# Flip before the scores, low parts before the maximum, three value passes in the forgetting attention

## The chip, the cores and the metric

The kernel runs on one core of a Trainium2 chip. The metric is the device time of one execution in microseconds; the time quoted is the median of the runs. All arithmetic is float32: TensorE (PE in the profile) reads float32 operands that are split by the program into a high part rounded to fp32r and a low part, the rest, and adds the products of the parts.

## The reference

One layer of a streaming encoder: half a SwiGLU block, a token mix with two groups of eight attention heads, and half a second SwiGLU block, with RMS norms around each. It runs on 1024 prompt rows and on 128 sample rows (8 streams of 16 with caches of 512). The change touches the two attentions of the prompt:

```python
s = einsum('bqhd,bkhd->bhqk', q, k) * scale        # scores of one head
if decay: s = s + (lq[t] - lk[s])                  # group B: forgetting attention (FoX)
s = where(mask, s, -inf)                           # block-causal (MLA) or per frame (FoX)
p = softmax(s, axis=-1)
out = einsum('bhqk,bkhd->bqhd', p, v)              # v has 64 columns per head
```

## The kernel before

The stages follow one another with a barrier between: feed-forward 1 with the input projection, latents, `mla_prompt`, `sample_setup`, `sample_attention`, `fox_prompt`, output projection, feed-forward 2. Each stage is five instruction lists written out by hand (PE; ACT, the scalar engine; DVE, the vector engine; POOL, GpSimd; SP, the sync engine for DMAs). Each engine works through its list in order, and semaphores tie the lists together.

`mla_prompt` (L1459) and `fox_prompt` (L1774) have the same skeleton. A head has PT = 8 row tiles of 128 queries. Row g = 8·n + t is tile t of head n; being causal, it has t + 1 key tiles. The parts of a row are:

- `score(g)` on PE writes the scores into one of two PSUM buffers; it waits for the exponentials of row g - 2, which read the same buffer.
- `maximum(g)` on DVE takes the row maximum, `exponent(g)` on ACT the exponentials into `p` (the one ACTIVATE of L1635 and L1955, with its sum read out after it).
- `flip_row(g)` on PE transposes `p` tile by tile into the two PSUM buffers of `flip`, in groups of at most four tiles (tiles 4 to 7 of a head have two groups); group x waits for `pt_lo` of group x - 2, its buffer's last reader.
- `weights_high(g)` on ACT copies a group out of PSUM as the high part, and `weights_low(g)` on DVE subtracts it from PSUM to give the low part.
- `prep`, `high`, `low` turn and split the queries and keys of head n + 1, one piece at each of t = 1, 2, 3, 4 (`PREP_STEP`). In `fox_prompt` POOL copies each high part a second time (`double`).
- `values(n, h, ...)` on PE multiplies the transposed weights of half h by V: half 0 of head n at t = 6, 7, half 1 at t = 0 to 3 of the next head. The stationary operand `vv` holds V's high and low parts side by side (128 columns), so two passes (weights high, weights low) give both in one PSUM bank: high·V in partitions 0 to 63, low·V in 64 to 127. ACT copies the upper half out (`take_low`), DVE adds it to the lower (`copy_out`), at t = 0 and t = 4.

The order around the change, in the loop over g (L1603, L1635 on; L1928 on in `fox_prompt`), LEAD = 2:

```
PE :  score(g+2)    flip_row(g)      prep, values
DVE:  maximum(g+2)  weights_low(g)   low, copy_out, invert
ACT:  weights_high(g)  exponent(g+2) high, v_high, take_low
```

In the last head of `fox_prompt`, at t = 0, ACT also issues the eight DMAs of `load_w_out`.

Of the kernel before, what the change touches and what calls it, by code (L numbers as in the profile page):

```python
# [8 lines left out]
P = 128  # L9
# [45 lines left out]
def plain(ap):  # L55

    return ap.bitcast(F32)
# [176 lines left out]
H = 8  # L234
# [1224 lines left out]
def mla_prompt(nc, ident, ident_bf, mask_bf, q_rows, kv_rows, krope, acc, early_hi, early_lo, inverse_out, load_next, limit):  # L1459
# [8 lines left out]
    with Tools(nc, "mla") as k:  # L1468
# [43 lines left out]
        with k.block() as block:  # L1512
# [17 lines left out]
            def _(pe):  # L1530
# [72 lines left out]
                keys(1)  # L1603
                for g in range(-LEAD, ROWS):
                    n, t = divmod(g, PT)
                    if g + LEAD < ROWS:
                        score(g + LEAD)
                    if g >= 0:
                        flip_row(g)
                        if n + 1 < H and t in PREP_STEP:  # L1610
                            prep(n + 1, PREP_STEP[t])
                        if n and t in PV_LATE:
                            values(n - 1, 1, PV_LATE[t])
                        if t in PV_EARLY:
                            values(n, 0, PV_EARLY[t])
# [65 lines left out]
            @block.vector  # L1681
            def _(dve):
                def low(n, r):
                    src, hi, lo, factor = part(n, r)
                    dve.wait_ge(hi_ok, PREP * n + r + 1)
                    dve.scalar_tensor_tensor(lo, src, factor, plain(hi), ALU.mult, ALU.subtract).then_inc(lo_ok, 1)

                def key_low(hf):
                    cols = slice(hf * HALF, hf * HALF + HALF)
                    dve.wait_ge(key_hi, hf + 1)  # L1690
                    dve.tensor_tensor(kT_lo[0][NOPE:QW, cols], key_bank(hf), plain(kT_hi[0][NOPE:QW, cols]), ALU.subtract).then_inc(key_lo, 1)

                def maximum(g):
                    n, t = divmod(g, PT)
                    dve.wait_ge(scored, g + 1)
                    dve.tensor_reduce(nmax[:, g:g + 1], scores[:, g % 2, 0:(t + 1) * P], axis=AX.X, op=ALU.max, negate=True).then_inc(maxed, 1)

                def weights_low(g):
                    hi, lo, cols = weights(g)
                    for x, k0, k1 in groups_of(g):  # L1700
                        dve.wait_ge(pt_hi, x + 1)
                        dve.tensor_tensor(lo[:, k0:k1, cols], flip[:, x % 2, 0:(k1 - k0) * P].rearrange("p (k n) -> p k n", n=P), plain(hi[:, k0:k1, cols]), ALU.subtract).then_inc(pt_lo, 1)

                def invert(n):
# [12 lines left out]
                low(0, 1)  # L1717
                key_low(0)
                low(0, 2)
                low(0, 3)  # L1720
                key_low(1)
                for g in range(-LEAD, ROWS):
                    n, t = divmod(g, PT)
                    if g + LEAD < ROWS:
                        maximum(g + LEAD)
                    if g >= 0:
                        weights_low(g)
                        if n + 1 < H and t in PREP_STEP:
# [45 lines left out]
def fox_prompt(nc, ident, ident_bf, mask_bf, decay, rows, loaded, acc, v_parts, decayT, inverse_out, load_next):  # L1774
# [11 lines left out]
    with Tools(nc, "fox") as k:  # L1786
# [1 line left out]
        p = k.sb("p", [P, NP_ROWS, SEQ])  # L1788
        early_hi, early_lo = [k.sb(f"early_{n}", [P, HT, HALF], F32R) for n in ("hi", "lo")]
        late_hi, late_lo = [k.sb(f"late_{n}", [P, PT, HALF], F32R) for n in ("hi", "lo")]  # L1790
        vv, low_rows, o_raw, scale_rows = v_parts
        nmax, total = [k.sb(n, [P, ROWS]) for n in ("nmax", "total")]
        inverse = k.sb("inverse", [P, 2, PT])
        scores = k.ps("scores", [P, 2, SEQ])
# [1 line left out]
        turn = k.ps("turn", [P, HALF])  # L1796
        out = k.ps("out", [P, HALF])
        pT_hi, pT_lo = (early_hi[:, :, :], late_hi[:, :, :]), (early_lo[:, :, :], late_lo[:, :, :])
        out_of = (turn, out)
        turned, hi_ok, lo_ok, doubled = k.sem("turned"), k.sem("hi_ok"), k.sem("lo_ok"), k.sem("doubled")  # L1800
        ones_ok, decay_turned, decay_taken = k.sem("ones_ok"), k.sem("decay_turned"), k.sem("decay_taken")
        decay_in = [k.sem(f"decay_in{b}") for b in range(2)]
        scored, maxed, exped, inverted = k.sem("scored"), k.sem("maxed"), k.sem("exped"), k.sem("inverted")
        inverse_at, scale_in, o_copied = k.sem("inverse_at"), k.sem("scale_in"), k.sem("o_copied")
        flipped, pt_hi, pt_lo = k.sem("flipped"), k.sem("pt_hi"), k.sem("pt_lo")
        v_hi_ok, v_lo_ok, pv_ok, low_out, o_taken = k.sem("v_hi_ok"), k.sem("v_lo_ok"), k.sem("pv_ok"), k.sem("low_out"), k.sem("o_taken")

        def turn_bank(n, r):

# [20 lines left out]
        with k.block() as block:  # L1830
# [29 lines left out]
            def _(pe):  # L1860
# [43 lines left out]
                def values(n, h, pieces):  # L1904
                    b = n % 2
                    for c in pieces:
# [8 lines left out]
                        c0 = max(0, c - HT * h) * P  # L1915
                        dst = out_of[h][:, c0:HALF]
                        high, low = pT_hi[h][:, c, c0:HALF], pT_lo[h][:, c, c0:HALF]
                        pe.matmul(dst, vv[b][:, c, :], high, start=(c == 0), stop=False)
                        last = pe.matmul(dst, vv[b][:, c, :], low, start=False, stop=(c == HT * (h + 1) - 1))
                        if c == HT * (h + 1) - 1:  # L1920
                            last.then_inc(pv_ok, 1)

# [4 lines left out]
                    prep(0, r)  # L1927
                for g in range(-LEAD, ROWS):  # L1928
                    n, t = divmod(g, PT)
                    if g + LEAD < ROWS:  # L1930
                        score(g + LEAD)
                    if g >= 0:
                        flip_row(g)
                        if n + 1 < H and t in PREP_STEP:
                            prep(n + 1, PREP_STEP[t])
                        if n and t in PV_LATE:
# [6 lines left out]
            def _(act):  # L1943
# [19 lines left out]
                        act.wait_ge(flipped, x + 1)  # L1963
                        act.activation(hi[:, k0:k1, cols], flip[:, x % 2, 0:(k1 - k0) * P].rearrange("p (k n) -> p k n", n=P), ACT.Copy).then_inc(pt_hi, 1)

                def take_low(n, h):
                    act.wait_ge(pv_ok, 2 * n + h + 1)
                    if n or h:
                        act.wait_ge(o_copied, 2 * n + h)
                    act.activation(low_rows, out_of[h][VD:P, :], ACT.Copy).then_inc(low_out, 1)  # L1970

                def v_high(n):
                    if n >= 2:
                        act.wait_ge(pv_ok, 2 * (n - 1))
                    if n == 0:
                        act.wait_ge(loaded[1], 16)
                    act.activation(vv[n % 2][:, :, 0:VD], v_rows(n), ACT.Copy).then_inc(v_hi_ok, 1)

                for hf in range(HALVES):
                    act.wait_ge(decay_turned, hf + 1)  # L1980
# [3 lines left out]
                for g in range(-LEAD, ROWS):  # L1984
# [5 lines left out]
                    if g >= 0:  # L1990
                        if n + 1 < H and t in PREP_STEP:
                            high(n + 1, PREP_STEP[t])
                        if t == V_STEP:
                            v_high(n)
                        if n and t == EARLY_OUT_STEP:
                            take_low(n - 1, 0)
                        if n and t == LATE_OUT_STEP:
                            take_low(n - 1, 1)
                        if n == H - 1 and t == 0:
                            act.wait_ge(turned, PREP * H)  # L2000
                            load_next(act)
                for h in range(HALVES):
                    take_low(H - 1, h)

            @block.vector
            def _(dve):
# [20 lines left out]
                    dve.reciprocal(inverse[:, n % 2, :], total[:, PT * n:PT * n + PT]).then_inc(inverted, 1)  # L2027

                def copy_out(n, h):
                    dve.wait_ge(low_out, 2 * n + h + 1)  # L2030
                    if n:
                        dve.wait_ge(o_taken, 2 * n + h - 1)
                    dve.tensor_tensor(o_raw[:, h, :], out_of[h][0:VD, :], low_rows, ALU.add).then_inc(o_copied, 1)

                for b in range(2):
                    dve.memset(plain(q_tail[b][64:TAIL, :]), 1.0).then_inc(ones_ok, 1)
# [2 lines left out]
                    low(0, r)  # L2039
                for g in range(-LEAD, ROWS):  # L2040
                    n, t = divmod(g, PT)
                    if g + LEAD < ROWS:
                        maximum(g + LEAD)
                    if g >= 0:
                        weights_low(g)
                        if n + 1 < H and t in PREP_STEP:
                            low(n + 1, PREP_STEP[t])
                        if n and t == EARLY_OUT_STEP:
# [9 lines left out]
            def _(pool):  # L2058
# [12 lines left out]

                def v_low(n):
                    pool.wait_ge(v_hi_ok, n + 1)
                    pool.tensor_tensor(vv[n % 2][:, :, VD:2 * VD], v_rows(n), plain(vv[n % 2][:, :, 0:VD]), ALU.subtract).then_inc(v_lo_ok, 1)

                for r in range(PREP):
                    double(0, r)
# [668 lines left out]
def layer(nc, x_prompt, x_sample, cache_ckv, cache_krope, cache_fk, cache_fv, cache_logf, g1_pre, g1_post, w1_gu, w1_down,  # L2746
# [14 lines left out]
    with Tools(nc, "all") as k:  # L2761
# [55 lines left out]
        with Tools(nc, "mix") as m:  # L2817
# [46 lines left out]
            with Tools(nc, "dec_all") as d:  # L2864
# [5 lines left out]
                fox_prompt_rows = [fox_q.take("rows0", [P, PT, FW])] + [fox_kv.take(f"rows{n}", [P, PT, FW]) for n in (1, 2)]  # L2870
                sample_setup(nc, ident, q_rows[:, PT, :], select, setup_in, load_first_keys, own)
                sample_attention(nc, ident, ident_bf, mask_bf[:, 2 * P:2 * P + NEW], pair_pick[:, :], own, cache_ckv, cache_krope, cache_fk, cache_fv, fox_rows, ckv_out, acc, fox_prompt_rows, fox_loaded, keys_in, tri[:, :], ones[:, :], logf, decay)
                fox_v = Region(nc, "fox_v", xT_at + 2 * PT * FW * 4, 4 * PT * VD * 4 + HALF * 4)
                fox_o = Region(nc, "fox_o", xT_at + 63488, 2 * SEQ * 4)
                v_parts = [[fox_v.take(f"vv{b}", [P, PT, 2 * VD], F32R) for b in range(2)], fox_v.take("low_rows", [VD, HALF])[:, :], fox_o.take("raw", [VD, HALVES, HALF]), fox_o.take("scale_rows", [VD, SEQ])]
                decayT = nc.alloc_sbuf_tensor_at("decayT", [4 * H, SEQ], F32R, offset=places_end + PT * FW * 4)
                fox_prompt(nc, ident, ident_bf, mask_bf[:, P:2 * P], decay, fox_prompt_rows, fox_loaded, acc, v_parts, decayT,
                           inverse_rows[1], lambda eng: [load_w_out(eng, w_out, w_out_raw, c, w_out_at) for c in range(KD)])
# [53 lines left out]
```

## Time and profile before

| | us |
|---|---|
| median of 3 runs | 2577.03 (2576.94 to 2579.33) |
| the profiled execution's own time | 2577.59 |
| its span in the trace | 2575.8 |
| `mla_prompt`, first to last exponential | 1112.7 to 1285.1 |
| `fox_prompt`, first to last exponential | 1456.4 to 1635.5 |

| engine | busy us | share |
|---|---|---|
| PE (matmul) | 2349.7 | 91% |
| DVE | 1547.3 | 60% |
| ACT | 997.5 | 39% |
| POOL | 820.9 | 32% |

Busy shares are means over all the stages. The two feed-forward blocks are most of the span; the change lies in two stages of some 190 us each, whose own rows stand below.

### The profile page before, as it was taken

The page shows a single profiled execution, that of the slowest core. Times are in us where ns is not written, and L with a number is a line of the kernel's source. Part 1 is how long each engine was busy: PE and PEld are TensorE (multiplying, and loading weights), DVE is VectorE, ACT ScalarE, POOL GpSimd, SP SyncE. Part 2 cuts the span into 40 slices and gives each one's busy share as a digit, 9 for nine tenths or more (in the row PEclk, how much of TensorE's full clock was granted, in tenths as well). Part 3 has the DMA queues.
Part 4 walks back from the last instruction along what each step waited for, and adds up shares of the span by engine and source line. Part 5 has one row for each costly group of instructions (what it writes and reads, how often), then busy time and mean ns, then how long its engine had stood idle before and what let it go on. Part 6 is the DMA issues. An engine that isn't in the chain of part 4 may idle for free. (4 is left out here: it accounts for less than half of the span.)

```text
span 2575.8 us, 41219 instructions
## 1 busy us (share of the span) xinstructions
PE 2349.7 (91%) x14523; PEld 2108.0 (82%) x14523; DVE 1547.3 (60%) x2502; ACT 997.5 (39%) x2013; POOL 820.9 (32%) x647
## 2 busy tenths in 40 slices
PE   5999999999989999878889878796999999999985
PEld 4999999998867789767766666685999999998864
DVE  7766666655587223366643566666766666655565
ACT  6222222233454112466633366534322222233443
POOL 1544444434461000012221032223444444434452
PEclk8999999999999999899989888897999999999998
DMA  4444444367564221010054200223344444456663
GB/s 151 126 151 131 150 141 158 125 202 239 185 220 165 104 72 39 24 38 9 13 214 160 84 10 14 107 98 98 101 158 141 141 145 135 144 190 211 199 208 134
DMA packets 247809, 330.90 MB, mean 128 GB/s; under 512 B 34416, under 2 KB 141040, under 8 KB 245648
## 3 DMA queue, kind: packets, MB, share of 16 engines
q1 hardware_dynamic: 246544, 325.26, 38.4%
q10 hardware_dynamic: 1152, 4.19, 0.4%
q8 instruction: 63, 1.03, 0.2%
q14 instruction: 50, 0.41, 0.0%
HBM read 234.51 MB, written 94.75 MB: 128 GB/s over the span
## 5 line engine op out<-in xcount | busy, mean ns | idle before, releaser
L62 PE MATMUL ffn_bank<-x_hi,ffn_w_w_hi 128*128 128x256 f32 (+1 forms) x2464 | 736.0, 299 | 24.4 <-DVE x_lo L969 23.8
L63 PE MATMUL ffn_bank<-x_lo,ffn_w_w_hi 128*128 128x256 f32 (+1 forms) x2464 | 734.1, 298 | 0.0
L64 PE MATMUL ffn_bank<-x_hi,ffn_w_w_lo 128*128 128x256 f32 (+1 forms) x2464 | 734.0, 298 | 0.0
L62 PEld LDWEIGHTS ffn_bank<-x_hi,ffn_w_w_hi 128*128 128x128 f32 x2464 | 472.4, 192 | 27.0 <-DVE x_lo L969 26.2
L63 PEld LDWEIGHTS ffn_bank<-x_lo,ffn_w_w_hi 128*128 128x128 f32 x2464 | 472.7, 192 | 0.0
L64 PEld LDWEIGHTS ffn_bank<-x_hi,ffn_w_w_lo 128*128 128x128 f32 x2464 | 472.3, 192 | 0.0
L738 POOL TENSOR_TENSOR ffn_split_dn_lo<-ffn_in_dn_raw,ffn_split_dn_hi 128x512 fp32r<-128x512 f32 x176 | 250.7, 1429 | 289.1 <-ACT ffn_split_dn_hi L805 283.5
L724 POOL TENSOR_TENSOR ffn_w_w_lo<-gu_raw,ffn_w_w_hi 128x512 fp32r<-128x512 f32 x176 | 239.6, 1362 | 300.3 <-ACT ffn_w_w_hi L755 300.1
L1001 DVE TENSOR_TENSOR ffn_split_a_lo<-ffn_in_a_raw,ffn_split_a_hi 128x512 fp32r<-128x512 f32 (+2 forms) x176 | 218.5, 1257 | 176.2 <-ACT ffn_split_a_hi L807 176.1
L62 PE MATMUL ffn_bank<-ffn_split_dn_hi,ffn_split_a_hi 128*128 128x512 f32 x704 | 278.7, 396 | 22.8 <-DVE ffn_split_a_lo L1001 18.7
L724 POOL TENSOR_TENSOR ffn_w_w_lo<-ffn_w_s,ffn_w_w_hi 128x512 fp32r<-128x512 f32 x132 | 192.8, 1462 | 299.6 <-ACT ffn_w_w_hi L755 299.6
L63 PE MATMUL ffn_bank<-ffn_split_dn_lo,ffn_split_a_hi 128*128 128x512 f32 x704 | 276.5, 393 | 0.0
L64 PE MATMUL ffn_bank<-ffn_split_dn_hi,ffn_split_a_lo 128*128 128x512 f32 x704 | 276.3, 392 | 0.0
L755 ACT ACTIVATE ffn_w_w_hi<-ffn_w_s 128x512 fp32r<-128x512 f32 x132 | 83.4, 632 | 377.6 <-DVE ffn_w_s L915 298.4
L805 ACT ACTIVATE ffn_split_dn_hi<-ffn_in_dn_raw 128x512 fp32r<-128x512 f32 x176 | 110.9, 630 | 275.5 <-PE ffn_bank L64 223.5
L755 ACT ACTIVATE ffn_w_w_hi<-gu_raw 128x512 fp32r<-128x512 f32 x176 | 110.1, 627 | 276.2 <-PE ffn_bank L64 273.8
L62 PEld LDWEIGHTS ffn_bank<-ffn_split_dn_hi,ffn_split_a_hi 128*128 128x128 f32 x704 | 133.5, 190 | 58.8 <-POOL ffn_split_dn_lo L738 23.4
L960 DVE TENSOR_TENSOR ffn_w_a_st<-ffn_w_u,ffn_w_gate 128x320 f32<-128x320 f32 (+1 forms) x176 | 167.6, 991 | 0.1
L64 PEld LDWEIGHTS ffn_bank<-ffn_split_dn_hi,ffn_split_a_lo 128*128 128x128 f32 x704 | 133.7, 190 | 27.9
L63 PEld LDWEIGHTS ffn_bank<-ffn_split_dn_lo,ffn_split_a_hi 128*128 128x128 f32 x704 | 133.6, 190 | 27.1
L62 PE MATMUL ffn_bank<-in_hi,all_xT_hi 128*128 128x512 f32 (+2 forms) x360 | 131.3, 365 | 6.6 <-DVE all_xT_lo L181 6.6
L63 PE MATMUL ffn_bank<-in_lo,all_xT_hi 128*128 128x512 f32 (+2 forms) x360 | 130.7, 363 | 0.0
(420 smaller groups left out, 4031.0 us busy)
## 6 DMA issues: line engine op xcount, KB each, us to landing
gu_raw<-in_w_ffn_gu SPq DMA_DIRECT2D x88, 512.0 KB, 5.2
ffn_w_w_raw<-in_w_ffn_down SPq DMA_DIRECT2D x22, 1024.0 KB, 4.9
a_rows<-ffn_w_a_st SPq DMA_DIRECT2D x44, 512.0 KB, 2.8
t_rows<-ffn_w_w_raw SPq DMA_DIRECT2D x88, 256.0 KB, 2.3
s_rows<-ffn_w_a_st SPq DMA_DIRECT2D x88, 256.0 KB, 2.4
ffn_in_dn_raw<-in_w_ffn_down SPq DMA_DIRECT2D x88, 256.0 KB, 3.5
ffn_in_dn_raw<-t_rows SPq DMA_DIRECT2D x88, 256.0 KB, 2.8
ffn_in_a_raw<-s_rows SPq DMA_DIRECT2D x88, 256.0 KB, 3.0
```

The source lines that it names most:

```text
L62: pe.matmul(out, w_hi, x_hi, start=first, stop=False)
L63: pe.matmul(out, w_hi, x_lo, start=False, stop=False)
L64: return pe.matmul(out, w_lo, x_hi, start=False, stop=last)
L724: pool.tensor_tensor(w_lo[n][:, :, :], raw, plain(w_hi[n][:, :, :]), ALU.subtract).then_inc(w_lo_ok, 1)
L738: pool.tensor_tensor(dn_lo[e][:, :], dn_raw[r][:, :], plain(dn_hi[e][:, :]), ALU.subtract).then_inc(dn_lo_ok, 1)
L755: act.activation(w_hi[n][:, :, :], raw, ACT.Copy).then_inc(w_hi_ok, 1)
L805: act.activation(dn_hi[e][:, :], dn_raw[r][:, :], ACT.Copy).then_inc(dn_hi_ok, 1)
L960: dve.tensor_tensor(a_st[at.b][:, col:col + CW[c]], up[c][:, :], gate[c][:, :], ALU.mult).then_inc(prod_ok, 1)
L1001: dve.tensor_tensor(a_lo[e][:, c0:c1], a_raw[r][:, c0:c1], plain(a_hi[e][:, c0:c1]), ALU.subtract).then_inc(a_lo_ok, 1)
```

## The change

In both stages PE flips row g before it computes the scores of row g + 2, and DVE subtracts the low parts of row g before it takes the maximum of row g + 2. ACT's list keeps its order. In `fox_prompt` alone V's high and low parts get tensors of their own with 64 columns each; the value products are three passes (V high by weights high, V high by weights low, V low by weights high) into 64 partitions, `take_low` is gone, and `copy_out` copies from PSUM when the products are done. The small product low by low is no longer formed there.

```diff
@@ mla_prompt and fox_prompt, PE
                     n, t = divmod(g, PT)
+                    if g >= 0:
+                        flip_row(g)
                     if g + LEAD < ROWS:
                         score(g + LEAD)
                     if g >= 0:
-                        flip_row(g)
                         if n + 1 < H and t in PREP_STEP:
@@ mla_prompt and fox_prompt, DVE
+                    if g >= 0:
+                        weights_low(g)
                     if g + LEAD < ROWS:
                         maximum(g + LEAD)
                     if g >= 0:
-                        weights_low(g)
@@ fox_prompt, values
-                        pe.matmul(dst, vv[b][:, c, :], high, start=(c == 0), stop=False)
-                        last = pe.matmul(dst, vv[b][:, c, :], low, start=False, stop=(c == HT * (h + 1) - 1))
+                        pe.matmul(dst, v_hi[b][:, c, :], high, start=(c == 0), stop=False)
+                        pe.matmul(dst, v_hi[b][:, c, :], low, start=False, stop=False)
+                        last = pe.matmul(dst, v_lo[b][:, c, :], high, start=False, stop=(c == HT * (h + 1) - 1))
@@ fox_prompt, ACT: take_low and its four calls
-                def take_low(n, h):
-                    act.wait_ge(pv_ok, 2 * n + h + 1)
-                    if n or h:
-                        act.wait_ge(o_copied, 2 * n + h)
-                    act.activation(low_rows, out_of[h][VD:P, :], ACT.Copy).then_inc(low_out, 1)
@@ fox_prompt, DVE: copy_out
-                    dve.wait_ge(low_out, 2 * n + h + 1)
+                    dve.wait_ge(pv_ok, 2 * n + h + 1)
...
-                    dve.tensor_tensor(o_raw[:, h, :], out_of[h][0:VD, :], low_rows, ALU.add).then_inc(o_copied, 1)
+                    dve.tensor_copy(o_raw[:, h, :], out_of[h]).then_inc(o_copied, 1)
```

The rest of the diff names the two new tensors in `v_high`, `v_low` and `layer`.

## Rows read from the trace of the kernel before

**Rows 1.** Busy time by window: window, length, each engine's busy us (count), PEclk, DMA.
```profile
1110.00:1286.00 176.00, 146.71 (x907) 122.47 (x908) 120.61 (x209) 121.17 (x272) 34.23 (x24) 0.95 0.06 19
1456.00:1636.00 180.00, 141.13 (x807) 115.70 (x806) 118.49 (x205) 118.08 (x269) 48.51 (x50) 0.87 0.10 35
1591.50:1593.00 1.50, 1.50 (x8) 1.50 (x9) 0.29 (x2) 0.87 (x3) 1.42 (x2) 0.50 0.00 0
```
**Rows 2.** Waits from 1456 to 1636: who waited for whom, us, times, longest.
```profile
ACT fox_p L1955 <- DVE fox_nmax L2015: 27.8, 43, 2.2
PE fox_flip L1901 <- DVE fox_late_lo L2021: 22.3, 16, 3.0
```
**Rows 3.** Timeline, ACT, one head of fox_prompt: start, us, line, operation [idle before].
```profile
1569.62 0.36 ACT L1955 ACTIVATE fox_p<-fox_scores,fox_nmax 128x128 f32<-128x128 f32 x1
...
1573.46 0.47 ACT L1955 ACTIVATE fox_p<-fox_scores,fox_nmax 128x256 f32<-128x256 f32 x1
...
1574.79 0.58 ACT L1955 ACTIVATE fox_p<-fox_scores,fox_nmax 128x384 f32<-128x384 f32 x1 [0.48 <-DVE fox_nmax L2015]
...
1577.43 0.69 ACT L1955 ACTIVATE fox_p<-fox_scores,fox_nmax 128x512 f32<-128x512 f32 x1 [0.69 <-DVE fox_nmax L2015]
...
1580.30 0.80 ACT L1955 ACTIVATE fox_p<-fox_scores,fox_nmax 128x640 f32<-128x640 f32 x1 [0.24 <-DVE fox_nmax L2015]
...
1583.28 0.90 ACT L1955 ACTIVATE fox_p<-fox_scores,fox_nmax 128x768 f32<-128x768 f32 x1 [0.51 <-DVE fox_nmax L2015]
...
1584.17 0.58 ACT L1947 ACTIVATE fox_q_both<-fox_turn 64x512 fp32r<-64x512 f32 x1
1584.65 0.62 ACT L1977 ACTIVATE fox_v_vv<-fox_x_rows 128x512 fp32r<-128x512 f32 x1
...
1586.62 1.01 ACT L1955 ACTIVATE fox_p<-fox_scores,fox_nmax 128x896 f32<-128x896 f32 x1 [0.71 <-DVE fox_nmax L2015]
...
1590.70 1.11 ACT L1955 ACTIVATE fox_p<-fox_scores,fox_nmax 128x1024 f32<-128x1024 f32 x1 [0.98 <-DVE fox_nmax L2015]
...
1593.56 0.36 ACT L1955 ACTIVATE fox_p<-fox_scores,fox_nmax 128x128 f32<-128x128 f32 x1
```
**Rows 4.** Timeline of the same head, DVE and PE.
```profile
1577.85 0.40 PE L1918 MATMUL fox_out<-fox_late_hi,fox_v_vv 128*128 128x512 f32 x1
1578.09 0.40 PE L1919 MATMUL fox_out<-fox_late_lo,fox_v_vv 128*128 128x512 f32 x1
...
1584.78 0.68 DVE L2010 SCALAR_TENSOR_TENSOR fox_q_both<-fox_turn,fox_q_both 64x512 fp32r<-64x512 f32 x1 [0.94 <-ACT fox_q_both L1947]
...
1585.49 1.09 DVE L2015 TENSOR_REDUCE fox_nmax<-fox_scores 128x1 f32<-128x896 f32 x1
...
1591.41 1.73 PE L1901 MATMUL fox_flip<-all_ident,fox_p 128*128 128x128 f32 x7 [2.99 <-DVE fox_late_lo L2021]
```
**Rows 5.** Groups by form from 1456 to 1636: busy us, mean ns, idle before.
```profile
L2021 DVE TENSOR_TENSOR fox_late_lo<-fox_flip,fox_late_hi 128x512 fp32r<-128x512 f32 x37 | 25.3, 685 | 17.0 <-ACT fox_late_hi L1964 16.5
L1964 ACT ACTIVATE fox_late_hi<-fox_flip 128x512 fp32r<-128x512 f32 x37 | 21.9, 594 | 19.1 <-PE fox_flip L1901 18.9
...
L2021 DVE TENSOR_TENSOR fox_early_lo<-fox_flip,fox_early_hi 128x128 fp32r<-128x128 f32 x8 | 2.3, 282 | 0.0
...
L2015 DVE TENSOR_REDUCE fox_nmax<-fox_scores 128x1 f32<-128x128 f32 x8 | 2.2, 276 | 0.7 <-PE fox_scores L1893 0.7
```
**Rows 6.** Timeline, ACT, mla_prompt: row 7 of head 2, then rows 0, 1.
```profile
1174.61 1.11 ACT L1635 ACTIVATE mla_p<-mla_scores,mla_nmax 128x1024 f32<-128x1024 f32 x1 [0.99 <-DVE mla_nmax L1696]
...
1176.85 0.37 ACT L1635 ACTIVATE mla_p<-mla_scores,mla_nmax 128x128 f32<-128x128 f32 x1
...
1179.09 0.48 ACT L1635 ACTIVATE mla_p<-mla_scores,mla_nmax 128x256 f32<-128x256 f32 x1
```
**Rows 7.** Timeline, ACT, mla_prompt: row 7 of head 6, four heads later.
```profile
1266.12 1.11 ACT L1635 ACTIVATE mla_p<-mla_scores,mla_nmax 128x1024 f32<-128x1024 f32 x1 [0.99 <-DVE mla_nmax L1696]
```
**Rows 8.** Timeline, ACT's DMA issues in the last head of fox_prompt.
```profile
1623.60 3.00 ACTq L2626 DMA_DIRECT2D w_out_raw<-in_w_out  x6
```

More of the change, by code:

```diff
@@ L1790, in fox_prompt @@
         late_hi, late_lo = [k.sb(f"late_{n}", [P, PT, HALF], F32R) for n in ("hi", "lo")]
-        vv, low_rows, o_raw, scale_rows = v_parts
+        v_hi, v_lo, o_raw, scale_rows = v_parts
         nmax, total = [k.sb(n, [P, ROWS]) for n in ("nmax", "total")]
@@ L1798, in fox_prompt @@
         pT_hi, pT_lo = (early_hi[:, :, :], late_hi[:, :, :]), (early_lo[:, :, :], late_lo[:, :, :])
-        out_of = (turn, out)
+        out_of = (turn[0:VD, :], out[0:VD, :])
         turned, hi_ok, lo_ok, doubled = k.sem("turned"), k.sem("hi_ok"), k.sem("lo_ok"), k.sem("doubled")
@@ L1805, in fox_prompt @@
         flipped, pt_hi, pt_lo = k.sem("flipped"), k.sem("pt_hi"), k.sem("pt_lo")
-        v_hi_ok, v_lo_ok, pv_ok, low_out, o_taken = k.sem("v_hi_ok"), k.sem("v_lo_ok"), k.sem("pv_ok"), k.sem("low_out"), k.sem("o_taken")
+        v_hi_ok, v_lo_ok, pv_ok, o_taken = k.sem("v_hi_ok"), k.sem("v_lo_ok"), k.sem("pv_ok"), k.sem("o_taken")
         def turn_bank(n, r):
@@ L1929, in _ @@
                     n, t = divmod(g, PT)
+                    if g >= 0:
+                        flip_row(g)
                     if g + LEAD < ROWS:
@@ L1932, in _ @@
                     if g >= 0:
-                        flip_row(g)
                         if n + 1 < H and t in PREP_STEP:
@@ L1976, in v_high @@
                         act.wait_ge(loaded[1], 16)
-                    act.activation(vv[n % 2][:, :, 0:VD], v_rows(n), ACT.Copy).then_inc(v_hi_ok, 1)
+                    act.activation(v_hi[n % 2][:, :, :], v_rows(n), ACT.Copy).then_inc(v_hi_ok, 1)
                 for hf in range(HALVES):
@@ L1994, in _ @@
                             v_high(n)
[L1995 to L1998, printed above, removed]
                         if n == H - 1 and t == 0:
@@ L2001, in _ @@
                             load_next(act)
-                for h in range(HALVES):
-                    take_low(H - 1, h)
             @block.vector
@@ L2041, in _ @@
                     n, t = divmod(g, PT)
+                    if g >= 0:
+                        weights_low(g)
                     if g + LEAD < ROWS:
@@ L2073, in v_low @@
                     pool.wait_ge(v_hi_ok, n + 1)
-                    pool.tensor_tensor(vv[n % 2][:, :, VD:2 * VD], v_rows(n), plain(vv[n % 2][:, :, 0:VD]), ALU.subtract).then_inc(v_lo_ok, 1)
+                    pool.tensor_tensor(v_lo[n % 2][:, :, :], v_rows(n), plain(v_hi[n % 2][:, :, :]), ALU.subtract).then_inc(v_lo_ok, 1)
                 for r in range(PREP):
@@ L2872, in layer @@
                 sample_attention(nc, ident, ident_bf, mask_bf[:, 2 * P:2 * P + NEW], pair_pick[:, :], own, cache_ckv, cache_krope, cache_fk, cache_fv, fox_rows, ckv_out, acc, fox_prompt_rows, fox_loaded, keys_in, tri[:, :], ones[:, :], logf, decay)
-                fox_v = Region(nc, "fox_v", xT_at + 2 * PT * FW * 4, 4 * PT * VD * 4 + HALF * 4)
+                fox_v = Region(nc, "fox_v", xT_at + 2 * PT * FW * 4, 4 * PT * VD * 4)
                 fox_o = Region(nc, "fox_o", xT_at + 63488, 2 * SEQ * 4)
-                v_parts = [[fox_v.take(f"vv{b}", [P, PT, 2 * VD], F32R) for b in range(2)], fox_v.take("low_rows", [VD, HALF])[:, :], fox_o.take("raw", [VD, HALVES, HALF]), fox_o.take("scale_rows", [VD, SEQ])]
+                v_parts = [[fox_v.take(f"{n}{b}", [P, PT, VD], F32R) for b in range(2)] for n in ("hi", "lo")] + [fox_o.take("raw", [VD, HALVES, HALF]), fox_o.take("scale_rows", [VD, SEQ])]
                 decayT = nc.alloc_sbuf_tensor_at("decayT", [4 * H, SEQ], F32R, offset=places_end + PT * FW * 4)
```

1 line of the change is left out of this document (removed).

## The prediction

> **What bounds the kernel now.** I read the busy times by window first. Both attention stages keep PE at about 80% of the time, DVE and ACT at 65 to 70% each [rows 1]: no engine is full, so a chain through several engines sets the pace. Nothing beside these stages can take up a change: each ends in a barrier, and what they gain or lose is lost or gained in the total, one for one.
>
> The waits say which chain. ACT waits 27.8 us for the maximum in 43 places, and PE waits 22.3 us for low parts, up to 3.0 us at a time [rows 2]. The timeline of one head then gives the eight steps, each from the start of one exponential to that of the next: row 0 to 1 3.84, 1 to 2 1.33, 2 to 3 2.64, 3 to 4 2.87, 4 to 5 2.98, 5 to 6 3.34, 6 to 7 4.08, 7 to the next 0 2.86; sum 23.94 us [rows 3]. In the exponentials of rows 2 to 7 ACT waits for the maximum. The chain of step 5 to 6 can be read off: exponential at 1583.28, ACT's high part of the next head's queries at 1584.17, DVE's low part of it at 1584.78, the maximum at 1585.49, then the exponential at 1586.62 [rows 3, 4]. The flipped weights are not in it: ACT copies the high part of row g and goes on to `exponent(g+2)`, while DVE subtracts row g's low part beside that exponential. That is the overlap which the present order buys.
>
> Two steps are of another kind. Before row 6 is flipped PE stands still for 2.99 us, waiting for row 5's low parts, which are queued behind the 1.21 us maximum of row 7. Seven transposes then take 1.73 us and the granted clock is 0.50, the 1.2 GHz level [rows 1, 4]. The steps 7 to 0 and 0 to 1 run in that state: 2.86 + 3.84 = 6.70 us. The same steps in the multi-head latent stage at a head where the clock did not stay low are 2.24 + 2.24 = 4.48 us [rows 6]. So the low clock costs the forgetting stage 2.2 us a head. The latent stage has 22.88 us a head, from four heads between rows 7 of head 2 and head 6 [rows 6, 7].
>
> **The change, part by part.** *The order on PE.* Flipping row g ahead of the scores of row g + 2 lets ACT take the high part earlier, by the scores' 0.3 to 1.2 us (up to four matmuls of 0.24 from start to start [rows 4]; an estimate for the smaller ones). The scores come later by the transposes, 0.11 each at the full clock, an estimate from half of 1.73/7. Neither is on the new chain below except through it.
>
> *The order on DVE.* This is the costly edit. ACT's list still says high(g), exponent(g+2). DVE's now says low(g), maximum(g+2). So maximum(g+2) cannot start before ACT has copied high(g) and DVE has subtracted it, and exponent(g+2), which stands right behind high(g), waits for both. What ran side by side becomes one file: exponential, (next head's piece on ACT and DVE), high, low, maximum, exponential. Behind the waiting exponential ACT holds the next head's high piece and high(g+1), and for these wait DVE and, through its buffers, PE.
>
> I write this file out for a head. Instructions on ACT start 0.10 before the one in front ends (0.58 to 0.48 in the pair at 1584.17), on DVE 0.08 before; a hop between the two costs 0.03. An exponential with its read-out holds ACT for its own length. High parts: 0.28, 0.38, 0.49, 0.60 for 128 to 512 columns; low parts 0.28, 0.41, 0.55, 0.69, the inner ones on the straight line between the rows; the maximum 0.28 plus 0.134 for each further tile [rows 3, 4, 5].
>
> - 7 to 0: 1.11 + high 0.60 + hop 0.03 + low 0.61 + 0.47 + maximum 0.28 + 0.03 = 3.13
> - 0 to 1: 0.36 + 0.60 + 0.03 + 0.61 + 0.61 + 0.41 + 0.03 = 2.65
> - 1 to 2: 0.47 + 0.28 + 0.03 + 0.20 + 0.54 + 0.03 = 1.55
> - 2 to 3: 0.58 + 0.38 + 0.03 + 0.33 + 0.68 + 0.03 = 2.03
> - 3 to 4: 0.69 + piece high 0.58 + 0.03 + piece low 0.61 + low 0.47 + 0.81 + 0.03 = 3.22 (high runs beside the piece's low)
> - 4 to 5: 0.80 + 0.58 + 0.03 + 0.61 + 0.61 + 0.94 + 0.03 = 3.60
> - 5 to 6: 0.90 + piece 0.48 + V high 0.52 + high 0.60 + 0.03 + low 0.61 + 0.20 + 1.08 + 0.03 = 4.45
> - 6 to 7: 1.01 + 0.58 + 0.03 + 0.61 + copy_out 0.61 + low 0.61 + 0.33 + 1.21 + 0.03 = 5.02
>
> The sum is 25.65 us, against 23.94: 1.7 more in the forgetting stage, although it has no slow PE in it yet. Steps 3 to 7 lose 3.0 (16.29 for 13.27), steps 7 to 1 win 0.9 and steps 1 to 3 0.4.
>
> *What stays of the low clock.* PE's stop ahead of row 6 does not go. Row 6 waits for low(5), which now stands before the maximum but behind exponential 6 on ACT, the piece, both high parts and copy_out: PE has nothing left after the scores of row 0, about 3 us again. So I expect the half clock after it, as now. But PE has slack there: row 6's transposes end about 1 us before ACT is free for their high part. Of the 2.2 us I keep 1.0 in the forgetting stage (bounds: 0 if the slack takes all, 2.2 if none). A head is 26.6, or 2.7 more than before.
>
> *The latent stage* has the same file, and keeps `take_low`. At step 2 to 3 that puts ACT's 0.6 and DVE's copy_out behind each other, 0.8 more: 26.45, against 22.88: 3.6 more a head. Bounds on the clock there: 0 and again 2.2, if the stop, 2.7 now, gets longer and the clock stays down as long as in the other stage; I take 0 because the slack covers the short form of it.
>
> *Three value passes.* A head has 4608 columns of weights in each pass (1280 for half 0, 3328 for half 1). At 0.24 for 512 the third costs PE 2.1 us a head, 17 in all [rows 4]. The cover is PE's own idle time: 141 us busy in 180 [rows 1] is 18.8 in a head of 23.94, so 21 in one of 26.6. I count 0 inside and 1 at the end of the stage, where the last half runs alone; without the cover it would be 17. Taking `take_low` out relieves ACT of 16 copies of 0.6 (9.5 us). At t = 4 it is worth nothing, for DVE's piece and copy_out stand in the file anyway; at t = 0 it is the 0.8 that the latent stage has and this one has not, which the sum holds already. The new copy I cost as the addition that it replaces; bounds 0.3 to 0.7 for each of 16, of which 8 are in the file: 0 to -3.
>
> *The ends.* The last head has no pieces, but its low parts go into the file: 0.2 + 0.33 + 0.47 + 0.61 + 0.81 + 0.94 for t = 0 to 5, 3.4 us, of which I take 3. In the forgetting stage ACT issues the eight loads there, six of them in 3.00 us [rows 8]; before, the stall of ACT had DVE's maximum done beside it, now high, low and maximum follow it: 1.5 more.
>
> *Sum.* Forgetting stage: 7 heads by 2.7 = 19, the last head 3 + 1.5, the value tail 1: 24. Latent stage: 7 by 3.6 = 25, the last head 3: 28. Together 52. On the profiled execution's own 2577.6 (span 2575.8) that is 2629.6; the median of the runs lies 0.6 lower, so 2629.
>
> **The rivals.**
> *PE spends more of each head at the low level.* For it: in the forgetting stage the mean clock is 0.87 already [rows 1], and in the new order PE is idle for a larger part, 21 of 26.6 us busy (0.79) there and about 19.5 of 26.45 (0.74, now 0.83) in the latent stage. Against: stops of under 1 us, of which both kernels have several a head, leave the clock alone at present. At the half rate PE's matmuls of a step go above the file's length; if the low stretch doubles, each head pays the whole 2.2 again in both stages: 15 by 2.2 = 33 above my sum, 2662. The Trainium skill, TensorE: Matmul & The Clock Gate, Part 1, says that the throttled state is the default and that activity releases it; by that rule an emptier PE speaks for this rival. Here the rows agree with it as far as one stop of 2.99 us and the 0.50 behind it go, and show nothing of a PE that is merely less busy.
>
> *The order is neutral and the third pass is bare.* If DVE's two jobs only change places in a cycle that PE bounds, then the reordering costs nothing, and the 17 us of matmuls come on top: 2577 + 17 = 2594. Against it stand the waits of ACT for the maximum; PE is never what they end on.
>
> *The other side: faster.* One mechanism: the stop before row 6. In the new order low(5) no longer waits for the 1.21 us maximum of row 7. If the stop shrinks from 2.99 to under 2 us, and with it the low clock goes, steps 7 to 1 fall to 4.5 us: 2.2 by 7 = 15 in this stage, and 1 by 7 in the latent one (an estimate: its mean clock of 0.95 lies less than half as far below full as the other's 0.87 [rows 1]), 2577 - 22 = 2555. It decides only if low(g) ahead of the maximum costs ACT nothing, that is if high(g) were early enough to have low(g) done before the scores of g + 2. At t = 5 high(5) stands on ACT behind exponential 6 and a piece, so the low parts cannot be early; I give it little.
>
> **How the numbers follow.** The file as forecast: 0.80. More low clock: 0.10. Neutral order with a bare pass: 0.05. Faster: 0.03. No change, the edits evening out: 0.02. A measurement of this kernel tells 0.2%, 5 us, from no change. Faster 0.03, same 0.02, slower 0.95. Range: the lower bounds (no clock cost in the forgetting stage, 7 less; the cheaper copy, 3; half a microsecond a head of work that hides after all, 8) give 2611; the upper ones (2.2 for 1.0 there, 8; 2.2 in half of the latent heads, 8; the rival's further part) reach 2658. I set 2609 to 2660.
>
> **What would show it.** Right: in a head the steps 3 to 7 are longer by 0.3 to 1.1 each and the low part stands directly before the maximum on DVE; the wait of ACT for the maximum about doubles in both stages; steps 5 to 6 and 6 to 7 near 4.4 and 5.0; PE's stop ahead of row 6 is still there. Wrong: exponentials that start without waiting for the maximum, PE at over 90% in these stages (the neutral rival), a granted clock of 1.0 throughout a head (the faster one), or below 0.8 as a mean of the stage (the first one).

## The result and the profile after

The changed kernel takes 2629.4 us (2626.7 to 2631.3), the one before 2577.0: a ratio of 1.0205, 95% interval 1.0182 to 1.0228. The forecast was 2629.

The busy time by window, in the columns of [rows 1]: the latent stage, the forgetting stage, and 1.5 us behind the stop ahead of row 6 of a forgetting head.

```profile
1110.00:1320.00 210.00, 161.97 (x920) 133.44 (x919) 120.61 (x209) 118.48 (x273) 34.08 (x24) 0.88 0.06 17
...
1487.00:1690.00 203.00, 159.53 (x904) 120.06 (x904) 117.97 (x205) 105.26 (x255) 48.65 (x50) 0.87 0.09 31
1612.00:1613.50 1.50, 1.50 (x7) 0.89 (x7) 0.26 (x1) 1.50 (x4) 1.38 (x1) 0.50 0.00 0
```

Apart from the third value pass (PE has 904 instead of 807 instructions in the forgetting stage, 18 us more), the instructions are almost those of [rows 1], spread over more time: DVE's 120.6 us in the latent stage is the same number in 206 instead of 172 us. The mean granted clock of the latent stage fell from 0.95 to 0.88; the forgetting stage kept 0.87. The waits of the forgetting stage, as in [rows 2], then that of the latent stage:

```profile
ACT fox_p L1959 <- DVE fox_nmax L2007: 94.8, 64, 2.7
...
PE fox_flip L1903 <- DVE fox_late_lo L2013: 24.9, 22, 2.9
```
```profile
ACT mla_p L1636 <- DVE mla_nmax L1697: 88.0, 62, 2.1
```

Every exponential now waits for its maximum: 64 of 64 where it was 43, 94.8 us for 27.8; in the latent stage it is 88.0 us in 62 places, where it was 18.0 in 33. ACT's part of a head of the forgetting stage, against [rows 3]:

```profile
1614.63 0.37 ACT L1959 ACTIVATE fox_p<-fox_scores,fox_nmax 128x128 f32<-128x128 f32 x1 [1.04 <-DVE fox_nmax L2007]
...
1617.26 0.47 ACT L1959 ACTIVATE fox_p<-fox_scores,fox_nmax 128x256 f32<-128x256 f32 x1 [1.20 <-DVE fox_nmax L2007]
...
1618.81 0.58 ACT L1959 ACTIVATE fox_p<-fox_scores,fox_nmax 128x384 f32<-128x384 f32 x1 [0.82 <-DVE fox_nmax L2007]
...
1620.85 0.69 ACT L1959 ACTIVATE fox_p<-fox_scores,fox_nmax 128x512 f32<-128x512 f32 x1 [1.09 <-DVE fox_nmax L2007]
...
1624.17 0.79 ACT L1959 ACTIVATE fox_p<-fox_scores,fox_nmax 128x640 f32<-128x640 f32 x1 [1.70 <-DVE fox_nmax L2007]
...
1627.74 0.90 ACT L1959 ACTIVATE fox_p<-fox_scores,fox_nmax 128x768 f32<-128x768 f32 x1 [1.73 <-DVE fox_nmax L2007]
...
1632.17 1.01 ACT L1959 ACTIVATE fox_p<-fox_scores,fox_nmax 128x896 f32<-128x896 f32 x1 [1.79 <-DVE fox_nmax L2007]
...
1637.15 1.12 ACT L1959 ACTIVATE fox_p<-fox_scores,fox_nmax 128x1024 f32<-128x1024 f32 x1 [2.66 <-DVE fox_nmax L2007]
...
1640.26 0.37 ACT L1959 ACTIVATE fox_p<-fox_scores,fox_nmax 128x128 f32<-128x128 f32 x1 [1.03 <-DVE fox_nmax L2007]
```

The chain of step 6 to 7 of the head before, in the timeline, all engines:

```profile
1606.53 1.01 ACT L1959 ACTIVATE fox_p<-fox_scores,fox_nmax 128x896 f32<-128x896 f32 x1 [1.79 <-DVE fox_nmax L2007]
...
1607.53 0.58 ACT L1951 ACTIVATE fox_k_twice<-fox_turn 64x512 fp32r<-64x512 f32 x1
1608.01 0.85 ACT L1968 ACTIVATE fox_late_hi<-fox_flip 128x512 fp32r<-128x512 f32 x2
1608.14 0.68 DVE L2002 SCALAR_TENSOR_TENSOR fox_k_tail<-fox_turn,fox_k_twice 64x512 fp32r<-64x512 f32 x1 [1.64 <-ACT fox_k_twice L1951]
...
1608.75 0.67 DVE L2025 COPY fox_o_raw<-fox_out 64x512 f32<-64x512 f32 x1
1609.35 1.00 DVE L2013 TENSOR_TENSOR fox_late_lo<-fox_flip,fox_late_hi 128x512 fp32r<-128x512 f32 x2
1610.17 1.73 PE L1903 MATMUL fox_flip<-all_ident,fox_p 128*128 128x128 f32 x7 [2.85 <-DVE fox_late_lo L2013]
1610.28 1.21 DVE L2007 TENSOR_REDUCE fox_nmax<-fox_scores 128x1 f32<-128x1024 f32 x1
1611.52 1.11 ACT L1959 ACTIVATE fox_p<-fox_scores,fox_nmax 128x1024 f32<-128x1024 f32 x1 [2.66 <-DVE fox_nmax L2007]
```

It is the file of the forecast in its order: exponential, piece high, piece low, copy, low parts, maximum, exponential, 4.99 us. And PE still stops for 2.85 us ahead of row 6 (2.99 in [rows 4]), with the same seven transposes in 1.73 us behind it.

Where the 53 us are, from the starts of the exponentials: the latent stage, first to last, went from 172.4 to 206.2 (+33.8), the forgetting stage from 179.1 to 201.9 (+22.8). The stretch between the stages, nearly all of it code that the change leaves alone, was 3.1 shorter (171.35 to 168.26). In the other twelve traces it lies between 169.7 and 173.4, with 172.1 in `a_warm`, whose code there is that of the changed kernel: so the 3.1 are no more than one execution differs from another, and no gain of the change can be told.

### The profile page after: what moved, and what is told of

It reads as the page before. It is cut to its first block and busy times, and to the rows that moved or that the text cites. A ratio compares the mean times of both kernels' runs of the same rounds, so it can differ in the third digit from the quotient of the medians.

```text
span 2628.9 us, 41379 instructions
## 1 busy us (share of the span) xinstructions
PE 2375.8 (90%) x14619; PEld 2114.7 (80%) x14619; DVE 1547.3 (59%) x2502; ACT 980.4 (37%) x1997; POOL 823.1 (31%) x647
## 5 line engine op out<-in xcount | busy, mean ns | idle before, releaser
L64 PE MATMUL ffn_bank<-in_hi,all_xT_lo 128*128 128x512 f32 (+2 forms) x360 | 130.7, 363 | 0.0
```

What stands on the lines that cost most here:

```text
L64: return pe.matmul(out, w_lo, x_hi, start=False, stop=last)
```

## The experiments

Each set of runs has runs of the kernel before beside it (medians 2575.2 to 2575.7 in the four sets). "Steps" are medians over heads 1 to 6, from exponential to exponential, as in the forecast.

**DVE's list back.**

```diff
 a_dve_back, against the changed kernel, both stages
-                    if g >= 0:
-                        weights_low(g)
                     if g + LEAD < ROWS:
                         maximum(g + LEAD)
                     if g >= 0:
+                        weights_low(g)
```

> The changed kernel with DVE's list as before (maximum of row g + 2 ahead of the low parts of row g) in both stages; PE's new order and the three passes stay. Theory (one file through ACT and DVE): the low parts leave the file, the steps 3 to 7 of a forgetting head go back from 3.3, 3.6, 4.4, 5.0 to about 3.0, 3.0, 3.2, 4.1 us, and the time is near the kernel before: 2572 to 2588, with some of the low clock gone in the forgetting stage. Rival (PE's order does it, the scores being late behind the transposes): it stays above 2610.

Measured: 2604.7, ratio 1.0113 (1.0096 to 1.0130). Steps 3 to 7 of the forgetting stage are 3.01, 3.11, 3.35, 4.05. So DVE's order is 25 of the 53 us when it is taken back last, and the steps are the forecast ones; but 29 us stay, and the range that I gave is missed. The latent stage, whose clock stays up in heads 2 to 6 here, still takes 24.0 us a head, 2.2 more than `b_warm` below, whose clock is up too; step 1 to 2 is 2.24 instead of 1.45. The timeline of that step, latent stage:

```profile
1235.47 0.42 DVE L1697 TENSOR_REDUCE mla_nmax<-mla_scores 128x1 f32<-128x256 f32 x1 [1.10 <-PE mla_scores L1567]
...
1235.81 1.28 DVE L1703 TENSOR_TENSOR mla_late_lo<-mla_flip,mla_late_hi 128x512 fp32r<-128x512 f32 x2
1235.93 0.47 ACT L1636 ACTIVATE mla_p<-mla_scores,mla_nmax 128x256 f32<-128x256 f32 x1 [0.24 <-DVE mla_nmax L1697]
...
1236.64 0.30 PE L1576 MATMUL mla_flip<-all_ident,mla_p 128*128 128x128 f32 x1 [0.74 <-ACT mla_p L1636]
1236.69 0.43 PE L62 MATMUL mla_scores<-mla_kT_hi,mla_qT_hi 96*128 96x384 f32 x1
...
1237.58 0.56 DVE L1697 TENSOR_REDUCE mla_nmax<-mla_scores 128x1 f32<-128x384 f32 x1 [0.49 <-PE mla_scores L1567]
```

PE's new order has made a file of its own: the scores of row 2 stand behind the flip of row 0, which needs the buffer that DVE frees with the first low part of row 7 (1235.81 + 0.69 = 1236.50, 0.14 before the flip starts), and that stands behind the maximum of row 1. The profile puts PE's wait down to ACT, whose exponential of row 1 ends at about the same time, but the flip of row 0 does not need it.

**PE's list back.**

```diff
 a_pe_back, against the changed kernel, both stages
-                    if g >= 0:
-                        flip_row(g)
                     if g + LEAD < ROWS:
                         score(g + LEAD)
                     if g >= 0:
+                        flip_row(g)
```

> The changed kernel with PE's list as before (scores of row g + 2 ahead of the flip of row g) in both stages; DVE's new order and the three passes stay. Theory: nothing comes back, as the file runs through ACT and DVE alone; the high part is taken later by the scores, so 2627 to 2640. Rival (PE's order does it): 2580 to 2600.

Measured: 2641.7, ratio 1.0261 (1.0242 to 1.0281): 12 us slower than the changed kernel, just beyond the range. The rival is out: PE's order is not what costs, and under DVE's new order it even helps.

**The three passes alone.** The kernel before with `values`, `v_high`, `v_low` and `copy_out` of the changed one.

> The kernel before with only the three value passes, the split V tensors and the copy in place of the addition in the forgetting attention. Theory: 96 more matmuls and 17 us more of PE work lie in PE's idle time except where the clock is low and at the end of the stage: +1 to +5, 2578 to 2582. Rival (bare pass): +17, 2594. If the 16 copies that ACT no longer makes were in the way: 2570 or less.

Measured: 2572.9, ratio 0.9992 (0.9983 to 1.0002), no change that can be told, if any a small gain, and below the range that I gave. The bare pass is out. The step 7 to 0 of the forgetting stage is 2.37 for 2.86 us, the others as before within 0.2.

**The two orders alone.** The kernel before with both hunks of the order.

> The kernel before with only the two orders changed in both stages; the forgetting attention keeps two passes over 128 columns, ACT's copy of the low rows and DVE's addition. Theory: the file has ACT's copy and DVE's addition behind each other at step 2 to 3, 0.8 us a head more than the changed kernel, whose third pass it does not pay: +1 to +6 on 2629, 2630 to 2635. Rival (the third pass is a good part of the loss): 2612 to 2620.

Measured: 2642.1, ratio 1.0255 (1.0238 to 1.0272), 13 us over the changed kernel, where I had 1 to 6. Step 2 to 3 of the forgetting stage is 2.97 for 2.03, as written out, and step 0 to 1 3.11 for 2.77; that makes the stage 8.6 us longer, and the rest of the 13 lies outside it. So the three passes gain some 3 us beside the old order, which cannot be told from nothing, and 13 beside the new one, where ACT's copy stands in the file.

**DVE's new order in three rows.**

```diff
 b_dve234, against the kernel before, both stages
+                    if g >= 0 and t in (2, 3, 4):
+                        weights_low(g)
                     if g + LEAD < ROWS:
                         maximum(g + LEAD)
                     if g >= 0:
-                        weights_low(g)
+                        if t not in (2, 3, 4):
+                            weights_low(g)
```

> The kernel before with DVE's new order at t = 2, 3 and 4 alone, in both stages; PE's order, the passes and the other steps stay. Theory (one file through ACT and DVE, step by step, whatever PE does): only the steps 3 to 4, 4 to 5 and 5 to 6 grow, to 3.3, 3.6 and 4.4 us, the rest keeps its length; 2.1 us a head by 15 heads and some in the last ones: 2607 to 2614. Rival (the loss needs both new orders, or is given back at the next step, where the low part is already done): 2577 to 2595.

Measured: 2635.1, ratio 1.0231 (1.0215 to 1.0246): 60 us, more than the 53 of the whole change, where I expected 32 to 39. Steps 4 to 5 and 5 to 6 are 3.57 and 4.42 in both stages, to the hundredth those of the changed kernel. Step 3 to 4 is 3.98 in the forgetting stage and 4.32 in the latent one, instead of 3.3. Its timeline, forgetting stage:

```profile
1604.94 0.50 PE L1904 MATMUL fox_flip<-all_ident,fox_p 128*128 128x128 f32 x3
1605.38 0.63 PE L1871 MATMUL fox_turn<-all_ident,fox_x_rows 128*64 128x128 f32 x4
1605.48 0.49 ACT L1967 ACTIVATE fox_early_hi<-fox_flip 128x384 fp32r<-128x384 f32 x1 [0.88 <-PE fox_flip L1904]
...
1606.00 0.56 DVE L2024 TENSOR_TENSOR fox_early_lo<-fox_flip,fox_early_hi 128x384 fp32r<-128x384 f32 x1 [0.68 <-ACT fox_early_hi L1967]
...
1606.47 0.81 DVE L2018 TENSOR_REDUCE fox_nmax<-fox_scores 128x1 f32<-128x640 f32 x1
...
1607.32 0.79 ACT L1958 ACTIVATE fox_p<-fox_scores,fox_nmax 128x640 f32<-128x640 f32 x1 [1.36 <-DVE fox_nmax L2018]
```

With the old list on PE the flip of row 2 comes after the scores of row 4 and their predecessors, ACT stands 0.88 us for it, and the low part and the maximum follow. This wait is what PE's new order takes away. The rival, that both orders are needed for a loss, is out. The latent stage's low clock costs here too: step 0 to 1 is 4.08.

In `a_pe_back` the same step is longer as well (3.99 in the latent stage, 3.21 in the changed kernel), but that is the smaller part of its 12 us: its latent stage is 2 us longer, its forgetting stage 8, most of it in step 0 to 1 (3.72 for 2.77). In one head the clock is low there from 1566.6 to 1573.5, behind a stop of 1.9 us, and in the same head of the changed kernel from 1559.0 to 1562.4, behind one of 2.85. So a good part of what PE's new order saves is time at the low clock; what keeps the clock down longer is not shown.

**PE's new order in one row.** As `a_dve_back` suggests, `if g >= 0 and t == 0: flip_row(g)` ahead of the scores, and at its old place for the other rows, on the kernel before.

> The kernel before with PE's new order at t = 0 alone, in both stages. Theory for the 29 us that PE's new order cost with DVE's old one: the scores of row 2 now stand behind the flip of row 0, which waits for the first low part of row 7, which DVE has behind the maximum of row 1. So only step 1 to 2 grows, in the latent stage from 1.45 to 1.9 to 2.2 us, less in the forgetting stage, where the low clock has made the step before it long anyway; 3 to 10 us in all, 2579 to 2586. Rival (the cost lies in each row, in the scores coming later by the transposes): step 1 to 2 stays at 1.45, the time at 2573 to 2578.

Measured: 2581.7, ratio 1.0021 (1.0011 to 1.0031). Step 1 to 2 is 2.02 in the latent and 1.69 in the forgetting stage (1.45 and 1.33 before), steps 2 to 7 keep their length within 0.02. The file through PE is there, in that row. The kernel is 6 us slower for it, of the 29; the clock moved with it, to a mean of 0.93 for 0.95 in the latent stage and of 0.90 for 0.87 in the other, so the 6 us are not the price of the file alone. The rest of the 29 was read from the steps of `a_dve_back` and not tried one by one: in its latent stage steps 3 to 4, 5 to 6 and 6 to 7 are 0.2 to 0.3 longer than before, step 0 to 1 is 0.46 longer than in `b_warm`, and the first and last heads are longer.

**The stop ahead of row 6, filled with idle work.**

```diff
 b_warm (18) against the kernel before, a_warm (11) against the changed one
+                        if t == 6 and n + 1 < H:
+                            pe.wait_ge(lo_ok, PREP * (n + 2))
+                            for c in range(18):
+                                pe.transpose(turn[:, c % HT * P:c % HT * P + P], ident[:, :], ident[:, :])
                         flip_row(g)
```

> The kernel before; in heads 0 to 6 PE makes 18 transposes of the identity into the free bank while it stands ahead of row 6 (work whose result nothing reads). Theory (the stop of 2.7 to 3.0 us drops the clock, and only that makes the steps 7 to 0 and 0 to 1 long): the steps fall to 2.2 and 2.2 us in both stages, 15 us less in the forgetting stage and 7 less in the latent one, about 2555. Rival (these steps are long for another reason, the dummies come on top): 2577 or more.

> The changed kernel with 11 such transposes at the same place. Theory (the changed kernel has slack behind the stop, so the low clock costs it 0.5 us a head in the latent stage and 0.2 in the other): step 0 to 1 falls from 3.1 to 2.63, 2 to 5 us less, 2624 to 2628. Rival (the low clock is a good part of the 53 us): below 2615.

Measured: `b_warm` 2558.5, ratio 0.9940 (0.9922 to 0.9958), and 2557.0, ratio 0.9930 (0.9916 to 0.9943), in another set. The steps 7 to 0 and 0 to 1 are 2.24 and 2.24 in both stages, the others unchanged but for 1 to 2 of the forgetting stage (1.45 for 1.33). The stages by window:

```profile
1110.00:1278.00 168.00, 154.91 (x1033) 129.44 (x1031) 118.32 (x207) 119.51 (x272) 34.01 (x24) 1.00 0.07 19
1448.00:1618.00 170.00, 143.03 (x932) 115.59 (x931) 116.81 (x205) 116.67 (x269) 49.15 (x50) 0.98 0.11 37
```

The granted clock is 1.00 and 0.98 where it was 0.95 and 0.87, and 126 transposes a stage that nothing reads make the kernel 17 to 18 us faster. `a_warm` is 2628.6, ratio 1.0209 (1.0180 to 1.0237): nothing gained that can be told, though step 0 to 1 falls to 2.63 in both stages. The changed kernel has slack behind the stop. Its heads are then 25.67 us in the forgetting stage and 26.50 in the latent one (but for one of 27.27, in which the clock was low once more), the two sums at full clock being 25.65 and 26.45.

**The stop, shortened with real work, in two ways.** `b_fill`: `values(n, 0, (0, 1))` ahead of the flip of row 6, and in the forgetting stage `v_low` ahead of `normalise` on POOL. `b_pe5`: PE's new order at t = 5 alone. Both on the kernel before.

> The kernel before with real work in the stop: at t = 6 the first two value products of the head come ahead of the flip of row 6 in both stages; in the forgetting stage POOL makes V's low part ahead of the normalisation, so that they can run. Theory: the stop falls under 2.3 us and the clock stays at 2.4 GHz: steps 7 to 0 and 0 to 1 near 2.3 and 2.2, 2553 to 2562. Rival (the flips of row 6 are delayed by the products): 2577 or more.

> The kernel before with PE's new order in row 5 alone: flip of row 5, then the scores of row 7, so that PE has more left when it would stop. Theory: the stop falls to about 2 us, the clock stays up, and row 5 alone costs at most 0.2 us a head: 2555 to 2565. Rival (any piece of PE's new order costs as it did with the whole, some 2 us a head): 2585 or more.

Measured: `b_fill` 2566.3, ratio 0.9967 (0.9954 to 0.9980), half of what I expected; `b_pe5` 2574.3, ratio 0.9998 (0.9986 to 1.0009), nothing. The waits of `b_fill`, then of `b_pe5`:

```profile
PE fox_turn L1920 <- POOL fox_v_vv L2078: 13.7, 7, 2.0
```
```profile
PE fox_flip L1904 <- DVE fox_late_lo L2027: 25.4, 21, 2.0
...
PE mla_flip L1576 <- DVE mla_late_lo L1705: 22.1, 16, 2.0
```

The longest waits of `b_pe5`, 2.0 us, are those of the last heads. In the forgetting stage a stop of 1.96 us is left in `b_fill` and one of 1.4 to 1.9 us in `b_pe5`, and the clock still falls around it in six heads of seven and in four. In the latent stage the stop is 1.3 us in `b_fill`, with the clock low in two heads, and 1.6 in `b_pe5`, with the clock low in four. In the forgetting stage of `b_fill` it is POOL's subtraction of V that PE now waits for. My figure of a harmless stop, 2.3 us, was wrong, and the trace of the kernel before spoke against it already, in head 0 of its latent stage:

```profile
1128.82 0.89 PE L1576 MATMUL mla_flip<-all_ident,mla_p 128*128 128x128 f32 x4 [2.04 <-DVE mla_late_lo L1702]
```
```profile
1129.00:1132.50 3.50, 3.50 (x16) 3.21 (x15) 1.47 (x5) 1.76 (x6) 0.00 (x0) 0.51 0.00 0
```

The rival for `b_pe5` is out as well.

**Passes on top of the filled stop.** `b_warm_three` is `b_three_pass` with the 18 transposes.

> The kernel before with the 18 idle transposes ahead of row 6 and with the three value passes in the forgetting stage. Theory (what the three passes gain in the kernel before is less time at the low clock, as they keep PE busier): with the clock already up nothing is left to gain and a little PE work is bare: 0 to 5 us above the kernel with the transposes alone. Rival (ACT's 16 copies less are the gain): 3 us or more below it.

> The kernel before with the 18 idle transposes ahead of row 6 once more, as the base for the one with three passes: 2555 to 2561.

Measured: 2559.2 (2555.6 to 2560.4), ratio 0.9937 (0.9924 to 0.9951), against 2557.0 (2556.1 to 2559.5) for the transposes alone. With the clock up the three passes gain nothing. That agrees with their 3 us in the kernel before coming from a busier PE (the mean clock of its forgetting stage is 0.91 for 0.87), which the interval there does not secure. The version to keep is `b_warm`, with DVE and PE in their old order and two passes.

## Why the prediction was right

**The file on ACT and DVE** is right, and in the steps to about 0.1 us:

| step, forgetting stage | before | forecast | after |
|---|---|---|---|
| 7 to 0 | 2.86 | 3.13 | 3.11 |
| 0 to 1 | 3.84 | 2.65, and up to 1.0 for the clock | 2.77 |
| 1 to 2 | 1.33 | 1.55 | 1.55 |
| 2 to 3 | 2.64 | 2.03 | 2.03 |
| 3 to 4 | 2.87 | 3.22 | 3.33 |
| 4 to 5 | 2.98 | 3.60 | 3.57 |
| 5 to 6 | 3.34 | 4.45 | 4.42 |
| 6 to 7 | 4.08 | 5.02 | 4.98 |

`a_dve_back` and `b_dve234` show that DVE's order makes these lengths, and the second that three rows do it without the others.

**What stays of the low clock** was placed wrong. I kept 1.0 us a head for it in the forgetting stage and none in the latent one. Heads 1 to 6 took 25.88 and 26.95 us; with the clock up behind the stop (`a_warm`) 25.67 and, in five heads of the six, 26.50. So it is 0.2 and 0.45. In the latent stage the clock did stay down longer, as the upper bound there had it, but not for the reason given: the stop did not get longer, it is 2.46 us for 2.66. A head before, then one after, from the fall of the clock:

```profile
1152.90:1156.30 3.40, 3.40 (x16) 3.12 (x15) 1.69 (x4) 1.26 (x5) 0.00 (x0) 0.51 0.03 4
1156.40:1159.80 3.40, 3.19 (x20) 2.51 (x18) 1.95 (x4) 2.85 (x8) 0.00 (x0) 1.00 0.28 82
```
```profile
1159.60:1163.00 3.40, 2.52 (x10) 1.84 (x10) 1.64 (x5) 2.07 (x4) 0.00 (x0) 0.50 0.01 2
1163.00:1166.40 3.40, 3.40 (x17) 3.31 (x16) 1.82 (x4) 1.91 (x5) 0.00 (x0) 0.50 0.15 45
```

The changed kernel has further stops of 0.8 to 1.7 us in such a head, where the kernel before has none of over 0.7; that they keep the clock down is not shown. The slack took most of the cost. The two errors, 7 us forecast and some 5 measured, nearly cancel in the sum.

**The stages** came out as 23 for a forecast 24, and 34 for 28. Of the missing 6 in the latent stage some 3 are the heads (4.0 instead of 3.6 over the kernel before, by 7), 2 the last head (4.9 instead of 3) and 1 the first. In the forgetting stage the parts miss both ways: heads 1 to 6 grew by 2.2 instead of 2.7, the first by 4.5 instead of 2.7. The stretches outside the stages differ by some us from one execution to the next, whatever the kernel, and happened to take 3 back. That 2629 came out to the microsecond is therefore luck within some 5 us; the mechanism and the size of a head are not.

**The order on PE** was judged too simply. "Neither is on the new chain" holds in the changed kernel, but not by itself: PE's order with DVE's old one costs 29 us (`a_dve_back`, the three passes included), and with DVE's new one it saves 12 (`a_pe_back`). In the first the scores stand behind a flip that waits for DVE, in the second the flip stands behind the scores and ACT and DVE wait for it; the clock moves with both.

**Three passes**: hidden inside the stage, as counted. The cost at the stage's end is there on PE (the last half's products take 4.7 us for 3.4) but not in the time: from the last exponential to the last normalisation the stage takes 12.3 us after, 12.9 before. The products start 1.0 us earlier behind that exponential, ACT's copy behind them is gone, and POOL's first normalisation of the end, which waits for the DMA of the scale rows, starts 8.2 us behind it instead of 9.8. The copy from PSUM has 0.67 us for the addition's 0.68, so it is no gain.

**The last head**: 5.4 us in the forgetting stage for 4.5 forecast. Step 2 to 3, in which ACT issues the loads, is 5.92 us there, 4.32 before. The order is 1.2 of the 1.6: from the end of the issues to the exponential it takes 1.52 us, 0.33 before, and every run has one of these two values, by DVE's order at t = 1. The other 0.4 is the issues themselves, 3.9 us long before and 4.4 after, and 3.9 to 5.6 in the other runs whatever the order. The rows, as in [rows 8]:

```profile
1670.34 0.58 ACT L1959 ACTIVATE fox_p<-fox_scores,fox_nmax 128x384 f32<-128x384 f32 x1 [0.82 <-DVE fox_nmax L2007]
1670.35 1.12 ACTq L2619 DMA_DIRECT2D w_out_raw<-in_w_out  x2
1671.49 3.25 ACTq L2619 DMA_DIRECT2D w_out_raw<-in_w_out  x6
...
1676.26 0.69 ACT L1959 ACTIVATE fox_p<-fox_scores,fox_nmax 128x512 f32<-128x512 f32 x1 [1.09 <-DVE fox_nmax L2007]
```

**The signs that I named**: all but one came. ACT's wait for the maximum did not double but grew by 3.4 and 4.9 times: the file makes every exponential wait, and I had thought of the wide ones.

**The rivals.** The neutral order with a bare pass is out by `b_three_pass`. More low clock was true in the latent stage (0.95 to 0.88) and cost some 3 us. Its price in the prediction was too high in any case: seven heads of each stage have the stop, so 14 by 2.2 and not 15, and 7 by 1.0 of that was in the sum already. The faster one fails at its condition, the stop did not shrink; but its second half, that the clock behind the stop is worth some 20 us, is what `b_warm` gains (17 to 18). Two slips of the prediction changed nothing: four matmuls of 0.24 make 1.0 us, not 1.2, and the terms of the forgetting stage add up to 24.5.

## What to carry to other kernels

When two engines pass a buffer to and fro, write the three lists side by side for one step and ask of each pair which runs beside which: moving one instruction ahead of another on one engine can turn two parallel branches into a file, and its price here was about the moved instruction's length, step by step (0.5 to 1.1 us). Two reorderings must be judged together, since here one costs 29 us alone and saves 12 beside the other. And look at where TensorE stops, and at the clock behind it: idle work in the stops of 2.7 and 3.0 us gained 17 us in the kernel before, and nothing that can be told in the changed one, whose chain has slack behind them.

## What the runs showed of the hardware

- The 1.2 GHz level still came with a stop of PE of 1.4 to 2.0 us in most heads of the forgetting stage (`b_pe5`, `b_fill`), and with one of 1.6 us in four heads of the latent stage of `b_pe5`; I had taken 2.3 us as harmless. In the latent stage of `a_dve_back`, with stops of at most 2.0 us, the clock stayed up in heads 2 to 6, and in the latent stage of the kernel before it stayed up behind the stop of 2.67 us that ends at 1175.3. So the length of the one stop does not settle it.
- Transposes of the identity that nothing reads held the clock up: 0.98 for 0.87 in the forgetting stage, 1.00 for 0.95 in the latent one (`b_warm`). The Trainium skill, TensorE: Matmul & The Clock Gate, Part 1, says that activity releases the throttle; by that rule, useless activity does too, and here it did.
- A weight load of 64 columns takes 137 ns where one of 128 took 190, but the matmul of 512 columns behind it takes 395 ns in both, and the next starts 0.23 us behind it in both: three passes of 64 columns are half as dear again as two of 128. Two groups of the changed kernel, then one of the kernel before:

```profile
L1922 PE MATMUL fox_out<-fox_late_hi,fox_v_lo 128*64 128x512 f32 x35 | 13.8, 395 | 0.0
...
L1922 PEld LDWEIGHTS fox_out<-fox_late_hi,fox_v_lo 128*64 128x64 f32 x56 | 7.7, 137 | 3.7
```
```profile
L1919 PEld LDWEIGHTS fox_out<-fox_late_lo,fox_v_vv 128*128 128x128 f32 x56 | 10.6, 190 | 0.9
```
